# Leaving out the filler products between a residual stage and the products behind its norm

## The reference

```python
def rmsnorm(x, g):
    y = x * lax.rsqrt(jnp.mean(x * x, axis=-1, keepdims=True) + RMS_EPS)
    return y * g

x = x + sqrelu_mlp(h, ff_w1[l], ff_w2[l])       # down0, down1
hk = rmsnorm(x, kv_norm_g); kvf = hk @ kvf_w    # norm "fox" behind down0, "ffa" behind down1
h = h + FFN_RES * g1 * swiglu(u, ...)           # dn1
u = modulate(rmsnorm_2(h, norm_mix), sh2, sc2)  # norm "mixn" behind dn1
h = h + g2 * token_mixing(u, ...)               # out
u = modulate(rmsnorm_2(h, norm_ff2), sh3, sc3)  # norm "ffb" behind out
h = h + FFN_RES * g3 * swiglu(u, ...)           # dn2
return rmsnorm_2(h, norm_final)                 # norm "final2" behind dn2
```

## Time and profile before

| | |
|---|---|
| median of 3 runs | 1444.61 us (1443.86 to 1446.01) |
| profiled execution | 1445.08 us, of which the span of instructions is 1443.3 us |
| TensorE busy | 1415.2 us (98% of the span) |
| VectorE busy | 1111.8 us (77%) |
| ScalarE busy | 691.0 us (48%) |
| filler matmuls (L740) | 210 |

### The profile page before, as it was taken

How to read it: one execution, slowest core, us unless ns; L and a number is a source line. 1 busy time by engine, 2 the same in 40 slices (tenths; PEclk the granted TensorE clock), 3 DMA queues, 4 the chain that set the end, 5 groups by cost and what they waited for, 6 DMA issues and landing times.

```text
span 1443.3 us, 21870 instructions
## 1 busy us (share of the span) xinstructions
PE 1415.2 (98%) x8580; PEld 1246.1 (86%) x8580; DVE 1111.8 (77%) x1660; ACT 691.0 (48%) x899; POOL 31.5 (2%) x20
## 2 busy tenths in 40 slices
PE   7999999999999999999999999999999999999997
PEld 6878998888889888888888988888988889888887
DVE  3799876698777787758886779997577678798654
ACT  2321664554434554645554355554453357556442
POOL 0000000000000000000000000000024200000000
PEclk9999999999999999999999999999999999999999
DMA  7444663355776455525558757757554426476451
GB/s 264 143 166 154 249 218 118 117 197 196 253 274 219 154 187 189 209 87 176 189 193 281 260 185 274 282 191 246 199 212 146 168 95 217 162 274 215 133 180 66
DMA packets 60192, 279.31 MB, mean 194 GB/s; under 512 B 6632, under 2 KB 8105, under 8 KB 35274
## 3 DMA queue, kind: packets, MB, share of 16 engines
q1 hardware_dynamic: 56248, 270.69, 53.4%
q10 hardware_dynamic: 3858, 7.45, 1.5%
HBM read 273.89 MB, written 4.19 MB: 193 GB/s over the span
## 4 chain that ended last, share of the span: by engine, by line
PE 85%; DMA 6%; DVE 6%; ACT 1%; issue 1%; DVEq 0%; SPq 0%; ACTq 0%
PE acc L476 36%; PE acc L478 18%; PE acc L497 10%; DMA ada_w<-in_ada 6%; PE acc L635 2%; PE acc L535 2%; PE acc L536 2%; PE acc L537 2%; PE stat L720 2%; DVE wsplit L1750 2%; DVE ada_w L2139 1%; PE acc L639 1%; PE stat L832 1%; PE turned L740 1%; PE score L1053 1%
## 5 line engine op out<-in xcount | busy, mean ns | idle before, releaser
L476 PE MATMUL acc<-hA,wsplit 128*128 128x512 f32 x1664 | 590.0, 400 | 2.7 <-DVE x L1835 1.1
L1175 ACT ACTIVATE wsplit<-raw 128x2048 fp32r<-128x2048 f32 (+3 forms) x214 | 381.1, 1782 | 193.9 <-PE acc L478 145.1
L1750 DVE TENSOR_TENSOR wsplit<-raw,wsplit 128x2048 fp32r<-128x2048 f32 (+3 forms) x214 | 455.0, 2129 | 16.1 <-ACT wsplit L1175 16.0
L478 PE MATMUL acc<-hA,wsplit 128*128 128x256 f32 x1664 | 464.6, 279 | 0.0
L476 PEld LDWEIGHTS acc<-hA,wsplit 128*128 128x128 f32 x1664 | 312.7, 188 | 79.7 <-issue 4.0
L478 PEld LDWEIGHTS acc<-hA,wsplit 128*128 128x128 f32 x1664 | 313.9, 189 | 0.4
L476 PE MATMUL acc<-hid,wsplit 128*128 128x512 f32 x648 | 224.8, 390 | 0.0
L478 PE MATMUL acc<-hid,wsplit 128*128 128x256 f32 x648 | 182.8, 282 | 0.0
L1185 ACT ACTIVATE lowp<-acc 128x512 f32<-128x512 f32 (+1 forms) x118 | 69.0, 585 | 205.1 <-PE acc L478 177.3
L476 PEld LDWEIGHTS acc<-hid,wsplit 128*128 128x128 f32 x648 | 121.7, 188 | 25.4
L478 PEld LDWEIGHTS acc<-hid,wsplit 128*128 128x128 f32 x648 | 122.8, 190 | 0.0
(11 more groups left out here) (314 smaller groups left out, 2054.5 us busy)
## 6 DMA issues: line engine op xcount, KB each, us to landing
raw<-in_gu SPq DMA_DIRECT2D x44, 1024.0 KB, 4.9
ada_w<-in_ada SPq DMA_DIRECT2D x144, 256.0 KB, 4.8
raw<-in_up SPq DMA_DIRECT2D x32, 1024.0 KB, 4.9
raw<-in_down SPq DMA_DIRECT2D x32, 1024.0 KB, 4.9
raw<-in_dn SPq DMA_DIRECT2D x32, 704.0 KB, 4.1
raw<-in_pw SPq DMA_DIRECT2D x12, 1024.0 KB, 7.8
raw<-in_memk SPq DMA_DIRECT2D x8, 1024.0 KB, 4.9
raw<-in_memv SPq DMA_DIRECT2D x8, 1024.0 KB, 5.3
```

The lines of the kernel that those rows point to most:

```text
L476: nc.tensor.matmul(dst.rearrange("p (s t) -> p s t", s=2), w, h, start=start, stop=False, skip_group_check=True)
L478: return nc.tensor.matmul(dst[:, 0:T], lo_w, h[:, 0, :], start=False, stop=stop, skip_group_check=True)
L1175: nc.scalar.activation(wsplit[:, slot, 0, 0:elems_of(n)], raw[:, slot, 0:elems_of(n)], ACT.Copy).then_inc(S("w_hi"), 1)
L1750: V.tensor_tensor(wsplit[:, slot, 1, 0:e], raw[:, slot, 0:e], wsplit[:, slot, 0, 0:e].bitcast(F32), ALU.subtract).then_inc(S("w_lo"), 1)
```

## The change

The filler matmuls are left out at all five places, and with them their wait for `ident_bf`, which had been set long before. Nothing takes their place. The computation is the same.

```diff
-            def norm_sums(name, pairs=range(PAIRS), filler=0):
+            def norm_sums(name, pairs=range(PAIRS)):
...
                         elif tilewise:
-                            if filler:
-                                keep_clock(filler)
                             pe.wait_ge(S("norm_sq"), PAIRS * q + p + 1)
...
-            def keep_clock(n):
-                pe.wait_ge(S("ident_bf"), 1)
-                for _ in range(n):
-                    nc.tensor.matmul(turned[:, 0, :], ident_bf[:], mask_bf[:], start=True, stop=True)
...
-                norm_sums(norm, [LAST], filler=10)
-                if norm != "final2":
-                    keep_clock(40)
+                norm_sums(norm, [LAST])
```

## The result

| | before | after |
|---|---|---|
| median of 6 runs | 1445.01 us (1443.31 to 1446.52) | 1450.45 us (1449.03 to 1455.12) |
| profiled execution | 1445.08 us, span 1443.3 | 1449.28 us, span 1447.5 |
| TensorE busy | 1415.2 us | 1401.4 us |

The ratio is 1.0042, with a 95% interval of 1.0030 to 1.0054: 5.4 us slower by the medians, 6.1 by the ratio. The forecast was 3.8 us slower, 1448.4 us in a range of 1445.0 to 1452.0.

The account below looks back on a forecast made before the run. The prediction took TensorE, 98% busy, as the bound: 4.7 us lost to a fallen clock less 0.9 us of gains makes 3.8 us slower, 1444.6 + 3.8 = 1448.4 us. The range was 1445.0 to 1452.0 us.

Parts of the forecast that it names:

- What bounds the kernel: TensorE, busy 98% of the span: delaying it a microsecond delays the end by about that, unless it would have waited anyway.
- Gains of 0.9 us: Time saved without fillers: 0.14 us behind down0, 0.1 behind dn1, 0.64 behind out, 0 behind down1 and dn2.
- Behind down1 ... Gain 0: Behind down1 the ten fillers ended before the last square, as TensorE's 1.55 us idle showed, so removing them gains 0.
- The idle stretches: Without fillers TensorE idles from last sum to first product: 4.4 us behind down0, 4.6 down1, 4.7 dn1, 4.6 out.
- The clock falls at most of the four places: TensorE's clock falls behind most of down0, down1, dn1 and out, costing 2.9 to 6.3 us; chance 0.66.
- The choice of three quarters: Of a loss between 0 and 6.3 us from cold starts, 4.7 us was chosen, as a fall may be missing or short.
- the full price: All four cold starts in full: 1.9 us each behind down1 and out, 1.5 down0, 1.0 dn1, 6.3 us together.
- Rival 1: The clock holds through the idle stretches, if a fall needs more than about 4.7 us: 1443.7 us, chance 0.10.
- The price of a cold start: At least 3.7 us at half speed from the first product on lose 1.9 us, the upper price of a place.
- The 1.5 us priced behind down0: Cold, the large matmuls behind down0 take 3.0 us instead of 1.5 and the tiny ones still 0.86: 1.5 us lost.
- Rival 3, longer cold: TensorE stays at half speed up to twice as long as at the start: 1450 to 1456 us, chance 0.09.
- The 0.54 us of wait behind dn1: TensorE's 0.54 us wait for VectorE's next operand at 1043.21 covers as much of 1.5 us, leaving 1.0 us lost.

Follow-up runs that it names:

- more_down0: The kernel before with 60 instead of 40 filler matmuls behind down0 alone: 1.0021 (1.0010 to 1.0032), 3.0 us slower.
- more_out: The kernel before with 60 instead of 40 filler matmuls behind out alone: 1.0012 (1.0002 to 1.0023), 1.7 us slower.
- no_ten: The kernel before without the ten fillers between the two last sums at all five places, the forty kept: 0.9997 (0.9984 to 1.0010).
- twenty: The kernel before without the ten fillers and with twenty instead of forty behind the last sum: 1.0064 (1.0044 to 1.0085), 9.2 us slower.
- all_bare: The changed kernel run once more, against the kernel before: 1.0046 (1.0029 to 1.0062), 1451.19 us.
- bare_down0: The kernel before without its fifty fillers behind down0 alone: 1.0032 (1.0019 to 1.0046), 4.6 us slower.
- bare_dn1: The kernel before without its fifty fillers behind dn1 alone: 1.0031 (1.0017 to 1.0044), 4.5 us slower.

## Why the prediction was right or wrong

**Direction and range** held: 1450.45 us against 1445.0 to 1452.0, slower by more than 0.2%.

**What bounds the kernel** held. The single profile spoke against it at the end of down1; the timed delays of more_down0 and more_out passed on.

**Gains of 0.9 us** were too small. Three terms were seen in the profiles (0.1 behind down0, less than 0.1 behind dn1, 0.6 behind out with no idle time left ahead of the variance). But "Behind down1 ... Gain 0" rested on an accident, the 1.55 us of the earlier trace rows; where that wait is missing, the ten cost 0.7 us there, which makes some 1.5 us in all. In time, no_ten is 0.4 us faster, with an interval from 2.3 us faster to 1.4 us slower, which holds 1.5, 0.9 and also nothing.

**The idle stretches,** 4.4 to 4.7 us, were measured as 4.29, 4.63, 4.64 and 4.63.

**The clock falls at most of the four places:** it fell at all four in both profiles. The choice of three quarters, made for a fall that may be missing or short, made the forecast low against the measured 5.4 us; the full price, less the gains of the prediction, is the same 5.4. That this fits so well is in part luck: in the profile after, the four places lost 5.3 us and not 6.3, the gains were 1.5 and not 0.9, and with single places bare the losses were much larger.

**The reason given for it was too strong.** It was read as if an idle stretch had to reach some 3.2 us, as at the end of the program. The clock fell with 2.1 us in twenty and with 1.84 us at 564. Rival 1's condition, more than 4.7 us needed, was wrong by far.

**The price of a cold start,** 1.9 us, came from 9 matmuls against 19 in 3.7 us at the kernel's start. The granted clock reads 1.00 in both windows of the earlier trace rows; that the first one was cold is the author's estimate from the counts. Against the measured losses 1.9 us was of the right size where the next stage has large products, but high for a stretch of 3.4 us (1.4 us and 1.4 us in the profile after; 2.1 and 2.4 with one place bare, where the stretch was 6.8 us and began in idle time). The large pairs take 1.7 times as long when cold, and not twice. The tiny matmuls were taken as not slowed; they are, from 0.11 to 0.17 us each in the profile after and to 0.21 while fully cold. The 1.5 us priced behind down0 came out as 1.5 by two errors that cancel: the large pairs lost 1.0 us instead of 1.5, the tiny ones 0.5 instead of nothing.

**Rival 3, longer cold,** was put at up to twice the length of the start and a chance of 0.09. Behind down0 and dn1 it is what happened in seven of eleven falls, in five of them beyond twice, with 10.2 and 13.7 us against 3.7. Its share of the result can't be told apart from chance, since the price of the places doesn't add up.

**The 0.54 us of wait behind dn1** did cover its share: 1.0 us was lost there in the profile after, as predicted.

**A loss of half the cold time,** on which the prices rest, agrees with the traces only roughly, and only for cold time that lies on products: in the profile after, 3.4 us of it cost 1.4 to 1.5 us, where half would be 1.7. The 6.8 us behind dn1 cost 1.0 us; 3.7 us of them were busy, and 0.54 us covered a wait.

## What to carry to other kernels

Where TensorE must wait for a norm and is the bound afterwards, products without a result in the gap can be worth their instructions, if they cover the gap up to the first real product and don't delay the step that the gap waits for; here the fillers at four places save 5 to 7 us, by the forty small bf16 ones at each, and the ten between the sums save nothing. A cover that stops short of the product can be dearer than none (the ten alone, 14 us slower), and where only part was covered, the fillers just ahead of the next product did better (3.2 against 9.2 us). A wait in one profile may be that execution's alone: before a delay is called absorbed there, put in a known delay and time it.

## What the runs showed of the hardware

- The profile counts the fillers as TensorE's work: x8580 before, x8370 on the page after, 210 fewer. Its rows overlap: a filler lasts 0.27 us there and starts 0.11 us behind the one before it (L740, before).
- The granted clock stayed at 0.50 for 3.4, 6.8, 10.2 or 13.7 us, the same kernel differing from one execution to the next (behind down0 3.4 us in the first profile of the change, 10.2 us in all_bare).
- In the stretches of 13.7 us TensorE was busy 11.6 of 13.5 us (bare_down0, bare_dn1), and in twenty all of them, each time at a granted clock of 0.50.
- In one execution of twenty the clock fell behind one idle stretch of 2.45 us and held behind another. Behind the wait of 1.84 us in the attention it fell in seven of fourteen profiles.
- Pairs of matmuls of 512 and 256 columns took 1.7 times as long at a granted clock of 0.50 as at 1.00 (four in 2.53 us against 1.49, the first 0.2 us still at 1.00).
- Matmuls of 16 and 32 columns start 0.21 us apart at a granted clock of 0.50 and 0.11 us apart at 1.00 (464.39, 464.60 and 464.82 in the first rows of the result; eight in 0.86 us in the earlier trace rows), so even these follow the clock.
